# Score rows in pairs, V products once a slot, dots and chunk outputs in larger groups, swapped compression, and a last tile added from its bank

## The reference, cut to what matters

```python
# block 1, nsa_mixer (8 heads in 2 groups, head width 64)
blk = kv[:, idx] + pe                       # 31 blocks of 32 tokens, for k and for v
hid = silu(einsum('bnlgd,ldh->bngh', blk, w1)); kc_or_vc = einsum('bngh,hd->bngd', hid, w2)
# per head: causal softmax over selected tokens and over the window (512 tokens: both plain causal here)
p = masked_softmax(q @ k.T * scale, mask, -1);  o = p @ v
out = g0 * o_cmp + g1 * o_sel + g2 * o_win  # g: sigmoid gates, 24 columns of the projection
x = x + (gate_pool * y_pool + gate_nsa * y_nsa) @ w_out, then a gated feed-forward with a short convolution
# block 2, two layers, each: index scores relu(iq @ ik.T) over 8 heads of width 64, top 128 of them,
# attention over those; differential attention (two softmaxes a head, p1 - lam * p2, head width 64);
# gated linear attention in chunks of 64 tokens: state = decay * state + k.T @ v, output = q @ state
```

## Time and profile before

| | before |
|---|---|
| median of 3 runs | 1949.58 us (1949.49 to 1950.72) |
| profiled execution, own time | 1950.57 us |
| its span | 1948.8 us |
| TensorE matmul busy | 1929.9 us, 99% of the span, 9837 matmuls |
| VectorE, ScalarE, GpSimd busy | 1159.9, 894.7, 342.5 us |
| DMA | 178.87 MB, mean 92 GB/s |
| granted TensorE clock | 1.0 |

### The profile page before, as it was taken

The page is one execution under the profiler, slowest core; times in us unless marked ns, Lnnn a source line. Parts: engine busy times, 40 slices in busy tenths (PEclk is TensorE's granted clock), DMA queues, the critical chain, the costliest instruction groups (busy, mean ns, idle before and its releaser), DMA issues.

```text
span 1948.8 us, 25508 instructions
## 1 busy us (share of the span) xinstructions
PE 1929.9 (99%) x9837; PEld 1559.7 (80%) x9837; DVE 1159.9 (60%) x1862; ACT 894.7 (46%) x1427; POOL 342.5 (18%) x172
## 2 busy tenths in 40 slices
PE   9999999999999999999999999999999999999999
PEld 7977777888888887788887787888788888788787
DVE  6867546585453557687555545466589545555443
ACT  5544455543333345533445454445443444545432
POOL 1010002211120122254010010232235110010211
PEclk9999999999999999999999999999999999999999
DMA  6211103223222333223122123224222212122321
GB/s 232 93 65 44 65 23 141 97 86 108 87 107 86 108 112 128 85 87 108 44 92 82 46 87 130 87 86 151 87 87 87 87 47 105 44 90 87 117 100 65
DMA packets 25735, 178.87 MB, mean 92 GB/s; under 512 B 2976, under 2 KB 3616, under 8 KB 5408
## 3 DMA queue, kind: packets, MB, share of 16 engines
q1 hardware_dynamic: 23904, 164.24, 23.4%
q10 hardware_dynamic: 1728, 13.24, 1.8%
HBM read 171.18 MB, written 6.29 MB: 91 GB/s over the span
## 4 chain that ended last, share of the span: by engine, by line
PE 94%; ACT 2%; DVE 2%; POOL 1%; DMA 1%; issue 0%; DVEq 0%; SPq 0%; ACTq 0%; POOLq 0%
PE pp L278 31%; PE pp L282 15%; PE pp L268 10%; PE pp L270 10%; PE pp L269 10%; PE po L278 3%; PE po L282 2%; PE po L805 1%; PE ps L1147 1%; PE ps L724 1%; PE pt L775 1%; PE ps L1098 1%; PE po L1082 1%; PE po L1034 1%; PE pt L1068 1%; DMA wraw<-weights 1%
## 5 line engine op out<-in xcount | busy, mean ns | idle before, releaser
L262 DVE TENSOR_TENSOR wlo<-wraw,whi 128x2048 fp32r<-128x2048 f32 x124 | 291.8, 2353 | 254.2 <-ACT whi L257 253.6
L257 ACT ACTIVATE whi<-wraw 128x2048 fp32r<-128x2048 f32 x150 | 286.3, 1909 | 48.5 <-PE pp L282 48.4
L278 PE MATMUL pp<-hhi,whi 128*128 128x512 f32 (+1 forms) x704 | 287.0, 408 | 1.0 <-DVE hlo L473 0.8
L278 PE MATMUL pp<-hlo,whi 128*128 128x512 f32 (+1 forms) x704 | 275.3, 391 | 0.0
L278 PE MATMUL pp<-whi,hhi 128*128 128x512 f32 x464 | 192.2, 414 | 0.0
L282 PE MATMUL pp<-hhi,wlo 128*128 128x512 f32 (+1 forms) x704 | 190.1, 390 | 0.0
L278 PE MATMUL pp<-whi,hlo 128*128 128x512 f32 x464 | 181.6, 391 | 0.0
L268 PE MATMUL pp<-split,whi 128*128 128x512 f32 x420 | 163.8, 390 | 0.0
L270 PE MATMUL pp<-split,wlo 128*128 128x512 f32 x420 | 163.4, 389 | 0.0
L269 PE MATMUL pp<-split,whi 128*128 128x512 f32 x420 | 163.4, 389 | 0.0
L1860 POOL TENSOR_TENSOR wlo<-wraw,whi 128x2048 fp32r<-128x2048 f32 x26 | 120.5, 4633 | 220.0 <-ACT whi L257 220.0
(11 more groups left out here) (419 smaller groups left out, 3476.9 us busy)
## 6 DMA issues: line engine op xcount, KB each, us to landing
wraw<-weights SPq DMA_DIRECT2D x150, 1024.0 KB, 4.8
out_t<-xT ACTq DMA_DIRECT2D x4, 1024.0 KB, 3.9
xT<-out_t ACTq DMA_DIRECT2D x2, 2048.0 KB, 8.7
wraw<-weights SPq DMA_DIRECT2D x4, 512.0 KB, 8.3
xT<-x_t SPq DMA_DIRECT2D x4, 512.0 KB, 8.8
work<-cmp_w ACTq DMA_DIRECT2D x1, 2048.0 KB, 7.5
xT<-x_t ACTq DMA_DIRECT2D x1, 2048.0 KB, 7.9
out_t<-xT SPq DMA_DIRECT2D x4, 512.0 KB, 2.6
```

The source lines that it names most:

```text
L257: nc.scalar.activation(whi[:, slot, :], wraw[:, slot, :], ACT.Copy).then_inc(w_hi, 1)
L262: nc.vector.tensor_tensor(wlo[:, slot, :], wraw[:, slot, :], whi[:, slot, :].bitcast(F32), ALU.subtract).then_inc(w_lo, 1)
L278: nc.tensor.matmul(out_ap, *pair, start=(start and n == 0 and part == 0), stop=False)
```

## The change

- Scores of query tiles 0 and 1 go together, side by side in one bank (`SC_AT`), in step 0, with their four masks behind; tiles 2 and 3 follow in steps 1 and 2, step 3 has none (slot 0: steps 0, 2, 3). Both attention stages. Maxima, exponentials, scalings and combinations are regrouped to match.
- The V products of a slot (block 1) run all together at the end of the slot after it.
- Index dots come in pairs after every second wide tile, the second of a pair in `pt`; the index gates' turn moves to after the first wide tile, and the second dot waits until VectorE has read it (`iw_kept`).
- Chunk outputs run two chunks at a time, ahead of the state products.
- Compression: the 62 block columns are stationary and w1 moves (128 columns), k and v in the two column halves; a turn brings the result back. Silu comes before the turn.
- Gates: 48 stationary columns (high and low of the same 24) take the place of two matmuls of three; the turn adds both (`C_TWO`), the sigmoid follows it. VectorE makes only the 24 low columns of that chunk.
- The last tile is added to x from its bank, in halves, and goes out in two pieces of 128 KB; tile 6 goes alone.

The diff, cut (ScalarE's and VectorE's loops for the last section, and the lines that only rename, are left out):

```diff
+SC_AT = (0, 128, 0, 0)
...
+        def hid_rows(kv):
+            return slice(64 * kv, 64 * kv + 2 * N_CMP)
...
+        def rows_in(s, u):
+
+            return ((0, 1), (), (2,), (3,))[u] if s == 0 else ((0, 1), (2,), (3,), ())[u]
+
         def pe_score_pair(pe, s, i):
 
-            t, b, w, n = s // 2, s % 2, P * (i + 1), 8 * s + 2 * i
-            if n >= 2:
+            t, b, w, n, at = s // 2, s % 2, P * (i + 1), 8 * s + 2 * i, SC_AT[i]
+            if n >= 2 and i != 1:
                 pe.wait_ge(ex_done, n)
             for x, y in ((0, 0), (0, 1), (1, 0)):
                 for g in range(2):
                     rows = y_rows(g)
-                    nc.tensor.matmul(ps[g][:, 0:w], qr[t % 2][x][rows, i * P:i * P + P], kr[b][y][rows, 0:w],
-                                     start=(x + y == 0), stop=False)
+                    nc.tensor.matmul(ps[g][:, at:at + w], qr[t % 2][x][rows, i * P:i * P + P], kr[b][y][rows, 0:w],
+                                     start=(x + y == 0 and i != 1), stop=False)
+
+        def pe_mask_pair(rows, at_mask):
+
             for g in range(2):
-                nc.tensor.matmul(ps[g][:, i * P:w], idb, msk[:, M_TRI:M_TRI + P], start=False,
-                                 stop=True).then_inc(sc_ready, 1)
-
-        def dve_max_pair(dve, s, i):
+                for i in rows:
+                    at = SC_AT[i] + i * P
+                    last = nc.tensor.matmul(ps[g][:, at:at + P], idb, msk[:, at_mask:at_mask + P], start=False,
+                                            stop=(i == rows[-1]))
+                last.then_inc(sc_ready, len(rows))
...
+        def bank_no(i, g):
+
+            return 2 * g + 2 if i < 2 else 2 * i + g + 1
+
+        def ex_no(i, g):
+
+            return 2 * g + i + 1 if i < 2 else 2 * i + g + 1
+
+        def dve_max_pair(dve, n, s, rows):
+
             for g in range(2):
+                dve.wait_ge(sc_ready, n + bank_no(rows[0], g))
+                for i in rows:
+                    last = nc.vector.tensor_reduce(pnmx[s % 2][:, 2 * i + g:2 * i + g + 1],
+                                                   ps[g][:, SC_AT[i]:SC_AT[i] + P * (i + 1)], AX.X, ALU.max, negate=True)
+                last.then_inc(mx_ready, len(rows))
+
+        def act_exp_pair(act, s, rows):
             for g in range(2):
+                act.wait_ge(mx_ready, 8 * s + bank_no(rows[0], g))
+                for i in rows:
+                    w, c = P * (i + 1), 2 * i + g
+                    nc.scalar.activation(p_buf(s, g)[:, OFF[i]:OFF[i] + w], ps[g][:, SC_AT[i]:SC_AT[i] + w], ACT.Exp,
+                                         bias=pnmx[s % 2][:, c:c + 1],
+                                         accum_out=psum_[s % 2][:, c:c + 1]).then_inc(ex_done, 1)
...
+        def dot_bank(p, g):
+
+            return (ps, pt)[p % 2][g]
+
         def pe_dots(pe, l, p):
 
             i, hp, e = 1 + p // 4, p % 4, 24 * l + 2 * p
             w = P * (i + 1)
             if p == 0:
                 pe.wait_ge(ix_parts, l + 1)
-            if e >= 2:
-                pe.wait_ge(ix_relu, e)
+            if e >= 4:
+                pe.wait_ge(ix_relu, e - 2)
...
-                if p == 1:
+                if p == 0:
                     pe.wait_ge(evac, section("ikg", l)[2] + 1)
                     for i in range(QT):
-                        last = nc.tensor.matmul(pt[0][:, 8 * i:8 * i + 8], alr_f[64:72, i * P:i * P + P],
+                        last = nc.tensor.matmul(pt[0][:, 480 + 8 * i:488 + 8 * i], alr_f[64:72, i * P:i * P + P],
                                                 ident[64:72, 64:72], start=True, stop=True)
                     last.then_inc(iw_turned, 1)
-                pe_dots(pe, l, p)
+                if p % 2 == 1:
+                    pe_dots(pe, l, p - 1)
+                    if p == 1:
+                        pe.wait_ge(iw_kept, l + 1)
+                    pe_dots(pe, l, p)
...
-                        pe_score_diff(pe, l, s, i)
+                        for row in rows_in(s, i):
+                            pe_score_diff(pe, l, s, row)
+                        if rows_in(s, i):
+                            pe_mask_pair(rows_in(s, i), M_CH)
...
+                for past in (c - 2, c - 1) if c >= 2 and c % 2 == 0 else ():
+                    i = past // 2
+                    pe.wait_ge(state_ready, 8 * l + past + 1)
+                    if past >= 2:
+                        pe.wait_ge(go_out, 8 * l + past - 1)
+                    for hd in range(4):
+                        rows, at = y_rows(hd % 2), P * (hd // 2)
+                        bank = D_BANKS[2 * (past % 2) + hd % 2]
+                        last = nc.tensor.matmul(bank[:, at:at + P], gq_f[rows, hd // 2, P * i:P * i + P],
+                                                st_f[past % 2][rows, hd // 2, :],
+                                                start=True, stop=True)
+                    last.then_inc(gla_o, 1)
...
+                        if s == 1 and i == 0:
+                            dve_combine(dve, l, 0, 3)
+                        if i == 1:
+                            dve_combine(dve, l, s, 0)
+                        if rows_in(s, i):
+                            dve_max_pair(dve, 4 * (U1 + 12 * l + 4) + 8 * s, s, rows_in(s, i))
                         if s == 0 and i == 0:
                             cz = section("cz", l)[0] + 1
                             dve_conv(dve, cz + 2, cz % 2)
-                    if s < 4 and i >= 1:
-                        dve_combine(dve, l, s, i - 1)
-                    if s >= 1 and i == 0:
-                        dve_combine(dve, l, s - 1, 3)
+                        if i == 1:
+                            dve_combine(dve, l, s, 1)
+                        if i == (3 if s == 0 else 2):
+                            dve_combine(dve, l, s, 2)
+                        if s > 0 and i == 3:
+                            dve_combine(dve, l, s, 3)
...
-                dve_next(dve, "wout2", l, lambda n, t: dve_add_x(dve, prod_f, n, t))
...
+                dve.wait_ge(mm_done, t0 + KT)
+                for half, signal in zip(HALVES, (x_half, x_ready)):
+                    nc.vector.tensor_tensor(xT[:, 7, half], xT[:, 7, half], pp[(par0 + 7) % 2][:, half],
+                                            ALU.add).then_inc(signal, 1)
...
+            pe.wait_ge(blk_ready, 2)
+            for x in range(16):
+                for kv in range(2):
+                    last = nc.tensor.matmul(ps[kv][hid_rows(kv), 0:P], blk_f[kv][:, x, :], w1_f[:, 16 * kv + x, :],
+                                            start=(x == 0), stop=(x == 15))
+                    if x == 15:
+                        last.then_inc(hid_done, 1)
+            pe_tm_tile(pe, "ksw", None, 0)
+            pe_tm_tile(pe, "ksw", None, 1)
+            pe.wait_ge(hid_silu, 2)
             for kv in range(2):
-                pe.wait_ge(blk_ready, kv + 1)
-                for x in range(16):
-                    last = nc.tensor.matmul(ps[kv][:, 0:2 * N_CMP], w1_f[:, 16 * kv + x, :], blk_f[kv][:, x, :],
-                                            start=(x == 0), stop=(x == 15))
-                last.then_inc(hid_done, 1)
-            pe_tm(pe, "ksw", None, 256)
-            pe.wait_ge(hid_out, 1)
...
-                    last = three(bank[0:24, :], (wh[:, x, 0:24], wl[:, x, 0:24]), (hhi[:, x, :], hlo[:, x, :]),
-                                 x == 0, x == KT - 1)
-                return last
+                    if x < KT - 1:
+                        nc.tensor.matmul(bank[0:48, :], wh[:, x, 0:48], hhi[:, x, :], start=(x == 0), stop=False)
+                    last = nc.tensor.matmul(bank[0:24, :], wh[:, x, 0:24], hlo[:, x, :], start=False, stop=False)
+                return nc.tensor.matmul(bank[0:48, :], wh[:, KT - 1, 0:48], hhi[:, KT - 1, :], start=False, stop=True)
...
-                last = nc.tensor.transpose(po[0][:, 24 * i:24 * i + 24], g_fm[0:24, i * P:i * P + P],
-                                           ident[0:24, 0:24])
+                last = nc.tensor.matmul(po[0][:, 24 * i:24 * i + 24], g_fm[0:48, i * P:i * P + P],
+                                        cst[0:48, C_TWO:C_TWO + 24], start=True, stop=True)
...
-                        pe_score_pair(pe, s, i)
+                        for row in rows_in(s, i):
+                            pe_score_pair(pe, s, row)
+                        if rows_in(s, i):
+                            pe_mask_pair(rows_in(s, i), M_TRI)
                         pe_tile_part(pe, "mg", None, 2 * s + i // 2, 2 * (i % 2), 4)
-                    if s >= 2 and i == 0:
-                        pe_pv_pair(pe, s - 2, 3)
...
-                        pe.wait_ge(ex_done, 8 * s + 2 * i + 2)
+                        pe.wait_ge(ex_done, 8 * s + min(2 * i + 4, 8))
                         nc.tensor.matmul(ps[i % 2][:, :], poolw[:, i, :], u_f[:, i, :], start=True,
                                          stop=True).then_inc(pool_mm, 1)
```

(55 more changed lines are left out.)

128 lines of the change are left out of this document (58 added, 70 removed).

## The result

| | before | after |
|---|---|---|
| median, 4 runs each | 1949.53 us (1949.39 to 1950.72) | 1924.61 us (1923.27 to 1925.71) |
| ratio | | 0.9871, 95% interval 0.9853 to 0.9888 |
| profiled execution, own time | 1950.57 us | 1923.27 us |
| its span | 1948.8 us | 1921.5 us |

The account below looks back on a forecast made before the run. TensorE's stream was taken to bound the kernel (94% of the chain), with a fixed cost per group of small matmuls. Terms -5.4 - 3.5 - 4.0 - 1.9 - 3.0 - 1.75 - 0.9 = -20.45 gave 1929.1 us, range 1923 to 1937.5.

Parts of the forecast that it names:

- Compression and gates: Swapped compression records 3.35 less, turns give back 0.4: -3.0; eight of 24 gate matmuls go, turn +0.1: -1.75.
- Dots: Index dots in both layers: 12 groups fewer at 0.42, -5.0; lone gates' turn +0.2, reader wait 0.3 a layer; -4.0.
- Chunk outputs: Three groups a layer joined, 6 times 0.32: -1.9, with no new waits.
- Differential attention: Both layers: paired scores -3.0, transposes no longer waiting for the last combination -0.5; -3.5 in all.
- -0.5 transposes waits: Differential attention: two transposes no longer wait for the last combination, now made first; -0.5.
- Pair stage: Block 1: paired scores -3.0, gathered V products -4.3, pooling waits +1.6, first-slot waits +0.3; -5.4 in all.
- the +1.6 of the sum: Block 1, slot 6: the wait of 0.78 behind the pooling products, no longer covered by V products, shows at two more steps.
- A: Joined groups save little: the joins give 7.5 in place of 17.2; 1938.8 us; chance 0.12.
- B: New waits: pairs' exponentials 0.5 late in 12 of 13 slots (+6), or VectorE's top-k chain (+2); about 1937; chance 0.12.
- E: Slower: scores wait for a whole pair's exponentials, 13 slots losing 1.9 each; 1953.5 us; chance 0.03.
- C: Gates: each change between 48 and 24 stationary columns costs 0.10, adding 1.5; 1930.6 us; counted inside the forecast's 0.62.
- D: More than counted: all upper ends of the joins and no wait in slot 0; about 1923 us; chance 0.08.

Follow-up runs that it names:

- order3: `u_scores` with one more edit: in the differential attention VectorE combines tile 3 at the end of its own slot; 1928.92 us.
- u_scores: Changed kernel with score rows one at a time again in both attention stages, VectorE's scalings and combinations at their old steps; 1932.05 us.
- u_pv: Changed kernel with block 1's V products spread over the steps again, score rows still in pairs; 1927.93 us.
- u_dots: Changed kernel with the index dots going out singly again, one group behind each tile of 12 matmuls; 1928.77 us.
- exps2: Changed kernel with two more 256-column exponentials on ScalarE ahead of the four of step 0 in every slot of block 1; 1926.19 us.
- exps6: Changed kernel with six more exponentials, about 2.2 us on ScalarE, ahead of the four of step 0 in every slot of block 1; 1937.75 us.
- one_half: Changed kernel with keys' and values' compression records in the same half of the stationary columns, in their two banks as before; 1928.85 us.
- turn_next: Changed kernel with the gates' turn put right before the first pair of dots in each layer (`p == 1` instead of `p == 0`); 1923.98 us.

## Why the prediction was right, and where its terms were off

The mechanism is the forecast one: TensorE's stream has a fixed cost for each group of small matmuls, the change has fewer groups, and nothing beside it came late enough to take it back. The forecast didn't come near by errors that cancel: all the larger ones have one sign, and the sum is short by 4.9. By steps, with the stage's measurement first:

- **Compression and gates**: -3.03 and -1.58 (-1.82 and +0.24 for the turn), forecast -3.0 and -1.75. Both sound; the turn as a product cost 0.24 instead of 0.1.
- **Dots**: -4.60, forecast -4.0. The join was right (0.43 for 0.42). The wait of 0.3 on the reader of the gates' turn did not exist: I had it held by a GpSimd conversion. In after it lies inside one (760.01, in a conversion from 759.38 to 763.96) and takes 0.19. The lone turn cost 0.26 (0.2).
- **Chunk outputs**: -2.54, forecast -1.9. The term was mis-sized: a join is worth 0.42, not 0.32. I had taken 0.87 less 0.55 for the joined group and overlooked that the group ahead of the state products falls too, from 0.64 to 0.55.
- **Differential attention**: -5.31, forecast -3.5. The joins at 0.37 stand (0.35). "-0.5 transposes waits" named the right cause, the last combination made first, but took it from the one listed wait, in slot 1. The same wait stood in slots 2 and 3, too short to be listed. `order3` measures it at 1.0 a layer.
- **Pair stage**: -7.12, forecast -5.4. The joined scores with the waits around slot 0 are as forecast: 2.14 come back in `u_scores`, and 0.48 are what slot 0 is shorter there than before the change, together 2.6 for 2.7. The mis-sized term is the V products. Between the kernel before and `u_scores` slots 1 to 8 fall by 4.50 although the pooling waits grow by 1.37 (0.97 to 2.34), so the products' share is 5.9, forecast 4.3; `u_pv` gives the same (4.49 and 1.37). Of these 1.6 more, 0.90 is the wait at the start of slot 2 on VectorE's scaling, which stands in the list of waits of before and in no term of my sum. About 0.45 are waits at the first transposes of the last slot and the full matmul behind them (1.30 before, 0.85 in `u_scores`), and the rest are changes of kind that I had counted for 8 groups. The pooling waits themselves were exact (3 x 0.78), but a wait of 0.19 in slot 7 went with them, which makes the +1.6 of the sum 1.37; the one in slot 0 was 1.52 for 1.9.
- **The end**: -1.16, forecast -0.9. The addition gave 0.50 (0.55), the small last piece 0.66 where I took 0.35 between 0 and 0.7.

Together the waits that stood in no term of the sum, or that it held and that did not come, make about 3.5 of the 4.9 that the stages gained beyond it (1.5 in the differential attention, 0.9 and 0.45 in the pair stage, 0.6 in the dots). Of the rest, 0.6 are the chunk outputs and 0.3 the small last piece; in the former I priced a group by itself and not by what stood before and behind it.

Of the rivals, A falls with `u_dots`, B and E with `exps2` and `exps6`, and C with the rows of the gates and with `one_half`. The top-k chain of B did come later, by 0.68 in layer 0: against the next attention's first turn its last operation starts 1.27 before it in the kernel before (906.04 and 907.31) and 0.59 before it in after (890.76 and 891.35). But that operation lies beside a GpSimd conversion and ends 0.28 after it in both, so what VectorE does next starts 2.05 after the turn in both (909.36, 893.40), and nothing was lost. D, the upper ends, came nearest: 1923 with a wait of 0 in slot 0. The 1.5 of that wait was there, so D's account isn't the true one either.

## What to carry to other kernels

Price a group of small matmuls by the period of the whole stream with and without it, not by its own rows: here 0.43 for dots, 0.42 for chunk outputs, 0.31 to 0.35 for narrow scores and 0.2 to 0.3 for V products, half of it or more in the neighbours. Price the parts together as well: pairing scores was worth 0.10 a slot without the gathered V products and 0.31 with them. When a wait is listed once in a loop, compare the same row in the loop's other turns; it may be there unlisted (0.43 against 0.22). And when work is gathered at the end of a step, look at what its pieces had covered: putting two of them back behind the pooling products, reordering three steps on VectorE, and dropping a wait that no score needed, gave another 5.7 us, beside 25 for the change.

## What the runs showed of the hardware

**A wait can cost more than its length.** In `exps6` TensorE idles for 3.03 us in slot 0. Behind it matmuls start 0.43 apart instead of 0.235 for six microseconds. The view of stretches (us, busy, count, granted clock, DMA) has the clock at its lower level, 0.50 or 1.2 GHz, after the idle time, and back at 1.00 after that:

```profile
114.00:117.00 3.00, 2.88 (x17) 1.00 0.00 0
117.50:121.00 3.50, 0.47 (x4) 0.88 0.00 0
121.00:124.00 3.00, 3.00 (x11) 0.50 0.03 5
124.00:127.00 3.00, 3.00 (x8) 0.50 0.00 0
127.00:130.00 3.00, 3.00 (x29) 1.00 0.00 0
```

So the 4.9 of that slot are 2.1 of waits and 2.8 of slow clock. Slot 6 of the same kernel has it again, with no long wait: two of 1.08 and 0.78, the second beginning 1.1 after the end of the first, then 3.4 us at the lower level, which are the 1.7 of slot 6:

```profile
236.00:239.60 3.60, 1.75 (x6) 1.00 0.21 30
239.60:243.00 3.40, 3.40 (x14) 0.50 0.71 282
243.00:246.00 3.00, 3.00 (x16) 0.99 0.00 0
```

Single waits of 0.98 (slots 2 to 5), 1.52 (after) and 2.24 (`exps2`, slot 0) left the clock at 1.00. At the start of the program a wait of 3.15 that ends at 10 us in `u_scores` has a clock of 0.71 to 0.72 in the six microseconds behind it, but one of 3.12 that ends at 10.4 us in `turn_next` has 1.00. The Trainium skill (TensorE: Matmul & The Clock Gate, Part 1) describes such a halving after idle time; by that rule, `exps6` (slot 0) and `u_scores` agree, while `turn_next` and slot 6 show that the length of one wait doesn't decide it. For rivals B and E it means that their price of one microsecond per microsecond holds only while the clock stays up.

**A GpSimd conversion held one VectorE operation and not another.** The last operation of the top-k chain (`TENSOR_SCALAR`, 128x512 f32 to bf16) takes 3.39 in the kernel before and 2.72 in after, and ends 0.28 after the conversion beside it both times, in layer 1 too; on 128x384, with no GpSimd work beside it, it takes 0.36 in after. The reader of the gates' turn, which reads PSUM, takes 0.19 inside such a conversion. What tells the two apart was not tested.

**Two column halves are worth nearly two.** 128 moving columns in one half cost 0.111 a record, in alternating halves 0.057 (3.64 over 64, fixed cost included), a factor of 1.96.
